# A decoder layer on one core: the feed-forward cut into four parts of 5, 5, 6 and 6 inner tiles in place of three of 8, 7 and 7

## What is computed

```python
x  = layer_norm(ALPHA * x + mix, ln1_g[l], ln1_b[l])
ff, nb = conv_ffn(x, w_up[l], conv_w[l], conv_b[l], w_down[l], buf[l])
x  = layer_norm(ALPHA * x + ff, ln2_g[l], ln2_b[l])

def conv_ffn(x, w_up, conv_w, conv_b, w_down, buf):
    up = x @ w_up                                   # 1024 -> 2 * 2816
    padded = jnp.concatenate([buf, up], axis=1)
    h = conv_b + padded[:, 0:T] * conv_w[0]         # causal, depthwise, width 3
    for j in range(1, CONV_W):
        h = h + padded[:, j:j + T] * conv_w[j]
    val, gate = jnp.split(h, 2, axis=-1)
    return (silu(gate) * val) @ w_down, padded[:, -(CONV_W - 1):]
```

## Time and profile before

| | us |
|---|---|
| median of three runs | 1313.35 |
| the three runs | 1312.7, 1313.35, 1317.45 |
| the profiled execution, its own time | 1313.02 |
| its span in the profile | 1311.3 |
| TensorE busy, matmul | 1269.4 |
| VectorE, ScalarE, GpSimd busy | 672.2, 437.3, 322.9 |

### The profile page before, as it was taken

How to read it: one execution, slowest core, us unless ns; L and a number is a source line. 1 busy time by engine, 2 the same in 40 slices (tenths; PEclk the granted TensorE clock), 3 DMA queues, 4 the chain that set the end, 5 groups by cost and what they waited for, 6 DMA issues and landing times.

```text
span 1311.3 us, 20499 instructions
## 1 busy us (share of the span) xinstructions
PE 1269.4 (97%) x8200; PEld 1229.8 (94%) x8200; DVE 672.2 (51%) x1126; ACT 437.3 (33%) x580; POOL 322.9 (25%) x195
## 2 busy tenths in 40 slices
PE   7999999999899999989999999999999999999997
PEld 7988879998889899989999999999999999999996
DVE  6786775656698546645454211355451124554334
ACT  5411112223547414643333200333331023333325
POOL 5200000000000044133333322233333223333653
PEclk9999999998999999989999999999999999999999
DMA  7431223425415500011112211111121101112212
GB/s 268 123 95 43 81 68 125 146 63 156 114 51 186 222 1 17 1 50 50 35 48 65 64 48 33 33 49 49 34 72 43 51 29 50 49 50 59 71 44 87
DMA packets 67883, 95.74 MB, mean 73 GB/s; under 512 B 23328, under 2 KB 47904, under 8 KB 67816
## 3 DMA queue, kind: packets, MB, share of 16 engines
q1 hardware_dynamic: 67824, 94.93, 23.6%
HBM read 75.54 MB, written 18.37 MB: 72 GB/s over the span
## 4 chain that ended last, share of the span: by engine, by line
PE 88%; DVE 6%; issue 3%; ACT 2%; POOL 1%; DMA 0%; ACTq 0%; SPq 0%; DVEq 0%; POOLq 0%
PE psum L1119 62%; PE psum L1409 6%; PE psum L1316 5%; PE psum L1189 4%; PE psum L1262 3%; PE psum L1240 1%; DVE SC L1725 1%; PE psum L1236 1%; PE psum L1224 1%; DVE K L1715 1%; DVE QP L1716 1%; DVE XL L1548 1%; PE psum L1200 1%; PE psum L1290 1%; PE psum L1291 1%
## 5 line engine op out<-in xcount | busy, mean ns | idle before, releaser
L1119 PE MATMUL psum<-XH,wh 128*128 128x344 f32 x1485 | 325.5, 328 | 16.5 <-DVE wl L1548 8.5
L1119 PE MATMUL psum<-XL,wh 128*128 128x344 f32 x1485 | 317.1, 322 | 0.0
L1119 PE MATMUL psum<-XH,wl 128*128 128x344 f32 x1485 | 315.2, 321 | 0.0
L1119 PEld LDWEIGHTS psum<-XH,wh 128*128 128x128 f32 x1485 | 249.6, 190 | 22.1 <-DVE XL L1548 9.8
L1119 PEld LDWEIGHTS psum<-XL,wh 128*128 128x128 f32 x1485 | 253.1, 190 | 0.0
L1119 PEld LDWEIGHTS psum<-XH,wl 128*128 128x128 f32 x1485 | 249.3, 189 | 0.0
L1913 DVE SCALAR_TENSOR_TENSOR hb<-ub,cp,hb 128x1024 f32<-128x1024 f32 x44 | 56.5, 1285 | 238.5 <-ACT hb L924 238.5
L1055 POOL TENSOR_TENSOR wl<-raw,wh 128x1024 fp32r<-128x1024 f32 (+1 forms) x44 | 115.7, 2630 | 256.2 <-ACT wh L928 227.1
L923 ACT ACTIVATE ub<-psum 128x1032 f32<-128x1032 f32 x44 | 45.5, 1034 | 206.1 <-PE psum L1119 151.7
L1916 DVE SCALAR_TENSOR_TENSOR hb<-ub,cp,hb 128x1024 f32<-128x1024 f32 x44 | 86.3, 1961 | 1.6
L1058 POOL TENSOR_TENSOR AL<-hb,AH 128x1032 f32 (+1 forms) x22 | 53.3, 2423 | 106.7 <-ACT AH L935 106.7
(11 more groups left out here) (310 smaller groups left out, 1944.4 us busy)
## 6 DMA issues: line engine op xcount, KB each, us to landing
raw<-in_w_up SPq DMA_DIRECT2D x44, 512.0 KB, 3.6
raw<-in_w_units SPq DMA_DIRECT2D x15, 512.0 KB, 4.6
raw<-in_w_dn SPq DMA_DIRECT2D x16, 448.0 KB, 3.4
fscr<-st SPq DMA_DIRECT2D x10, 516.0 KB, 2.9
R<-in_xT SPq DMA_DIRECT2D x8, 516.0 KB, 6.6
out_yT<-R SPq DMA_DIRECT2D x24, 172.0 KB, 1.9
raw<-in_w_dn SPq DMA_DIRECT2D x8, 512.0 KB, 3.6
WOR<-in_w_out SPq DMA_DIRECT2D x6, 512.0 KB, 6.9
```

The lines of the kernel that those rows point to most:

```text
L1119: ins = nc.tensor.matmul(psum[:, 3 * slot + b, 0:CW], w, x[:, k, CW * b:CW * b + CW], start=(first and p_ == 0), stop=(last and p_ == 2))
```

## The change

```diff
--- before.py
+++ after.py
@@ -44,7 +44,7 @@
 LN_EPS = 1e-5
 RMS_EPS = 1e-6
 F_FLOOR = 1e-20
-PARTS = [(0, 8), (8, 7), (15, 7)]
+PARTS = [(0, 5), (5, 5), (10, 6), (16, 6)]
 TWO_PI_1 = 6.28125
 TWO_PI_2 = 0.0019350051879882812
 TWO_PI_3 = 3.019916050e-07
@@ -386,7 +386,7 @@
         WOL = [sb(f"WOL{m}", [P, KD * P], F32R, p2) for m in range(2, KD)]
         WOH = [sb(f"WOH{m}", [P, KD * P], F32R, p2) for m in range(2, KD)]
         p2.close()
-        AH, AL = sb("AH", [P, PARTS[0][1], T], F32R), sb("AL", [P, PARTS[0][1], T], F32R)
+        AH, AL = sb("AH", [P, max(n for _, n in PARTS), T], F32R), sb("AL", [P, max(n for _, n in PARTS), T], F32R)
         ub = [sb(f"ub{i}", [P, 2 + T]) for i in range(2)]
         hb = [sb(f"hb{i}", [P, T]) for i in range(2)]
         sqacc = sb("sqacc", [P, NB - 1, CW])
```

## The result

The change takes 1327.68 us, the median of four runs (1325.49 to 1330.56), against 1313.05 for the kernel before in the runs beside it: a ratio of 1.0105, interval 1.0076 to 1.0134, or 13.8 us slower (10.0 to 17.6); the two medians differ by 14.6. The forecast was 1326.4 us.

The account below looks back on a forecast made before the run. The feed-forward was taken as bound by TensorE's matmul count, which the change leaves alone. Seams +6.9, LayerNorm +2.8 and clock +3.3 us make 13.0, so 1326.4 us from 1313.35; range 1320.0 to 1330.0.

Parts of the forecast that it names:

- The seams' cover: Turn from up- to down-projection: nk + 2 steps of 1.417 us cover the chain; seams of five cost 2.90 us each.
- The seam of six: Turn to down-projection after a part of six tiles: eight steps of cover against a 12.75 us chain, costing 1.75 us.
- The chain and its shortening: From ScalarE's copy to AL's end: narrower GpSimd splits shorten VectorE's wait, giving 12.48 us at five tiles, 12.75 at six.
- Rival 3: At narrow seams VectorE gets through before GpSimd's split: chain 11.2 us, no clock lost, +5.6 us, 1318.9 us; chance 0.06.
- The extra down pass: Additional down-projection pass: its evacuations, weight loads, copies and splits stay hidden; counted as nothing, bound 0 to 0.5 us each.
- The LayerNorm: Final LayerNorm beside the shorter last part: TensorE waits for GpSimd, +2.4 us at two variances, +0.4 at the last mean.
- The clock: Behind both seams of five idleness drops the granted clock to 0.50 for 3.3 us, 1.65 us each, +3.3 us together.
- rival 2: No fall of the clock behind any seam, the page's rule: 1323.1 us; chance 0.13.
- one fall fewer: Rival at the seams of five: the clock falls behind one only, 1324.7 us; chance 0.22.
- The sum: Whole kernel: seams 6.9, LayerNorm 2.8 and clock 3.3 us make 13.0 us more.

Follow-up runs that it names:

- e7: The change with GpSimd's split of each part's last second weight tile held back until VectorE's convolution is done; 1321.46 us, ratio 1.0048 against the kernel before.
- e6: The change with all of slot 1's steps but its last moved ahead of the waiting step; 1326.04 us, ratio 1.0078 against the kernel before.
- e1: The change with three parts of 8, 8 and 6 tiles in place of 5, 5, 6, 6; 1316.43 us, ratio 1.0012 against the kernel before.
- e2: The change with parts of 5, 5, 5 and 7 tiles in place of 5, 5, 6, 6; 1328.75 us, ratio 1.0108 against the kernel before.
- e3: The change with buffers AH and AL still allocated for eight tiles; 1325.67 us, ratio 1.0087 against the kernel before.
- e5: The change with GpSimd's seven additions of squares per column block made in one go; 1326.55 us, ratio 1.0088 against the kernel before.
- e12: The kernel before the change, unchanged, run and profiled once more; 1313.77 us, ratio 1.0003.
- e4: The change with 14 unused filler matmuls ahead of the waiting step at the seams of five; 1325.55 us, ratio 1.0085 against the kernel before.
- e11: The change with 3 unused filler matmuls ahead of the waiting step at the seams of five; 1325.21 us in one run.

## Why the prediction was right, point by point

**The seams' cover.** Right. TensorE's timeline at the first seam of the change:

```profile
656.72 0.63 PE L1119 MATMUL psum<-AH,wh 128*128 128x344 f32 x3
...
666.19 0.64 PE L1119 MATMUL psum<-AH,wl 128*128 128x344 f32 x3
669.39 0.74 PE L1119 MATMUL psum<-AH,wh 128*128 128x344 f32 x3 [2.57 <-POOL AL L1058]
669.97 0.76 PE L1119 MATMUL psum<-AL,wh 128*128 128x344 f32 x3
670.52 1.06 PE L1119 MATMUL psum<-AH,wl 128*128 128x344 f32 x3
```

Seven steps from 656.72 us end at 666.19 + 0.47, 1.420 us each (1.417 said). The second weight group comes at 669.97 in place of 667.13: the seam costs 2.84 us where 2.90 were worked out. The seam of six cost 1.74 (1.75 said).

**The chain and its shortening.** Right. From ScalarE's copy at 656.91 to 666.98 + 2.37 = 669.35 us it takes 12.44 us (12.48 said), at the seam of six 12.73 (12.75 said). VectorE's small operation at the first seam, and the splits by width, against the earlier trace rows:

```profile
660.44 1.53 DVE L1914 SCALAR_TENSOR_TENSOR hb<-cp,hb 128x8 f32<-128x8 f32 x1
```

```profile
L1068 POOL TENSOR_TENSOR wl<-raw,wh 128x640 fp32r<-128x640 f32 x12 | 18.8, 1568 | 54.9 <-ACT wh L950 54.9
...
L1068 POOL TENSOR_TENSOR wl<-raw,wh 128x768 fp32r<-128x768 f32 x6 | 11.1, 1847 | 31.7 <-ACT wh L950 31.7
```

2.15 ns a column held down to 640 columns: 1568 ns, where 1.58 us were worked out. e7 shows that this wait is the cause. Rival 3 needed VectorE to get through first; it never did in the change. The Trainium skill (SBUF — State Buffer, "Who interferes with whom") has a VectorE operation with two inputs in SBUF and a GpSimd operation that reads SBUF lock each other out, in the order of their start; both directions are in the rows of e7, the small operation free when the split comes later, the multiplication longer when the split comes first.

**The extra down pass.** Right to count nothing for it: a wait for weights appears behind no seam of the change. Its place right behind a seam is as tight as said, since one step fewer makes it wait (e6).

**The LayerNorm.** Right in mechanism, and slightly short. TensorE's second mean, its variance, the last mean; GpSimd's last squares and its last sum:

```profile
1291.97 0.74 PE L1418 MATMUL psum<-hb,ones_ln 128*128 128x344 f32 x2
...
1302.76 0.85 PE L1426 MATMUL psum<-sqacc,ones_ln 128*128 128x344 f32 x2 [0.95 <-POOL sqacc L1085]
...
1309.74 0.84 PE L1418 MATMUL psum<-hb,ones_ln 128*128 128x344 f32 x2 [0.47 <-POOL hb L1094]
1310.43 0.74 PE L1420 MATMUL psum<-R,ones_ln 128*128 128x344 f32 x2
```

```profile
1299.80 2.92 POOL L1085 TENSOR_TENSOR sqacc<-sqacc,ub 128x344 f32<-128x344 f32 x3
...
1308.77 0.92 POOL L1094 TENSOR_TENSOR hb<-hb,R 128x344 f32<-128x344 f32 x1 [3.99 <-DVE R L1957]
```

The variance stands 10.79 us behind the mean (10.85 said); the last mean 6.98 behind the variance (6.87) and its second matmul 7.67 (7.44). The whole term can be read from the last part, TensorE's first matmul in it in the change and in the kernel before:

```profile
1235.04 0.32 PE L1409 MATMUL psum<-AH,wh 128*128 128x344 f32 x1
```

```profile
1212.28 0.32 PE L1409 MATMUL psum<-AH,wh 128*128 128x344 f32 x1
```

To the end of the span it is 90.8 us with 432 matmuls of that line, and 99.0 with 504 before. 72 matmuls at 157.4 ns are 11.3 us, but only 8.2 went away: the term is 3.1 us, and 2.9 in e1, where 2.8 were worked out.

**The clock.** Right for this execution:

```profile
670.60:673.40 2.80, 2.80 (x12) 2.80 (x11) 1.23 (x1) 0.74 (x1) 0.96 (x1) 0.50 0.00 0
844.60:847.50 2.90, 2.90 (x12) 2.90 (x12) 0.54 (x1) 0.65 (x1) 0.00 (x0) 0.50 0.02 6
```

Two falls, at 1.55 us each where 1.65 was taken. The step that took both as the likeliest holds over the runs: behind idleness of 2.57 us the clock fell in 8 of 9 cases (the change, e2, e3, e5), behind the 1.48 us of the seams of six in none of six. My reading of the earlier trace rows was cruder than the runs allow, though, since it took one execution for the rule. The idle stretch of 1.30 us, behind which the clock had stayed at 1.00, is there again in the change, and so is that of 2.17, with the clock behind each:

```profile
371.09 2.00 PE L1262 MATMUL psum<-QP,K 128*128 128x64 f32 x16 [1.30 <-DVE QP L1716]
...
451.99 0.66 PE L1110 MATMUL psum<-XH,wh 128*128 128x344 f32 x1 [2.18 <-DVE XL L1548]
```

```profile
373.40:376.80 3.40, 3.40 (x16) 3.40 (x15) 3.30 (x6) 1.33 (x2) 0.00 (x0) 0.50 0.29 77
...
451.90:453.40 1.50, 1.23 (x3) 0.79 (x3) 1.46 (x4) 0.52 (x2) 0.00 (x0) 0.50 1.02 418
```

Some 2.3 us behind the 1.30 us the clock is low here; so it is in seven of the fourteen profiles, and in the other seven it is not. Behind the 2.17 us it fell in all fourteen, in the change even before TensorE took up work again. And in e12, in the same kind of stream as at the seams, it fell 1.5 us behind a wait of 1.75 us, where the thirteen other profiles have waits of 1.29 to 1.84 us and no fall:

```profile
35.34 0.74 PE L1119 MATMUL psum<-XH,wh 128*128 128x344 f32 x3 [1.75 <-POOL wl L988]
```

```profile
36.90:40.30 3.40, 3.40 (x14) 3.40 (x13) 3.40 (x2) 3.40 (x8) 2.63 (x1) 0.50 0.74 250
```

So the length of a stall alone does not settle it, and why 2.10 us brought no fall at two seams stays open. Two falls were the likeliest, and it is in part luck that this execution had just two. By the Trainium skill (TensorE: Matmul & The Clock Gate, "What's actually happening"), whose rule is rival 2 of the prediction, no seam would have cost anything in clock. The runs disagree with it.

**The sum.** 2 x 2.84 + 1.74 - 0.62 + 3.1 + 3.1 = 13.0 us, where the stretch shows 12.9. The mechanism is right term by term, but that forecast and stretch agree to 0.1 us is in part luck: the seams were put 0.1 us too high and the falls 0.2, the LayerNorm 0.3 too low, and one fall fewer, as at the third seam of e2, would have taken off 1.55. That the median of whole runs came out 1.3 us above the forecast is within its interval.

## What to carry to other kernels

When work is cut into more parts, count for each seam the steps that can run without the last piece, and set them against the chain that makes that piece: here the chain stayed at 12.4 to 13.3 us while the cover fell from 14.2 to 9.9. A stall of the matmul engine of some 2.6 us can cost half as much again in clock (1.55 us on 2.84 here), and filling the idleness (e4) or splitting it (e6, e7) kept the clock up at these seams. A single execution does not give a border for that: look at the same stall in several profiles. A part that hides a tail, as the last one hides the LayerNorm, must not be shortened without looking at the slowest helper in it.

## What was not expected of the hardware

- The half clock is not a matter of the idleness alone: at the seams 2.57 us let it fall in eight cases of nine, 1.63 and 2.10 us in none of four, while elsewhere it fell behind 1.75 us once (e12), behind 1.30 us in seven profiles of fourteen, and behind the 1.22 us of the last LayerNorm in one (e11).
- The same code ahead of the feed-forward ran with 17 to 27 us at half clock, and the first loop unit began between 562.2 and 567.4 us. The same kernel, before the change, took from 1307.85 to 1319.03 us in the runs beside e1. Its mean granted clock went with it: 0.994 and 0.995 in the two fastest executions, 0.986 in the slowest.
- GpSimd and VectorE lengthen each other's operations: the split of 640 columns takes 1.54 us alone, and 2.20 when it starts inside a VectorE operation (chain of the change, 659.75).
